# First feed-forward's down product: two by two blocks in seven products instead of eight, with the sums of blocks made on GpSimd during the up phase

## The reference

```python
h2 = rms_norm(x, norm2_g[l])
up = h2 @ w_up[l]                                  # 1024 -> 2 * 2816
up = causal_depthwise_conv(up, ffn_dw_w[l])        # 3 taps
gate, val = jnp.split(up, 2, axis=-1)
x = x + (jax.nn.silu(gate) * val) @ w_down[l]      # 2816 -> 1024
```

## Time and profile before

| | |
|---|---|
| median of 3 runs | 2790.98 us (2790.71 to 2793.44) |
| profiled execution, its time | 2792.19 us |
| its span | 2790.6 us |
| granted TensorE clock over the span | 0.993 |
| TensorE busy | 2728.8 us (98%) |
| VectorE busy | 1754.9 us (63%) |
| GpSimd busy | 642.3 us (23%) |

### The profile page before, as it was taken

How to read it: one execution, slowest core, us unless ns; L and a number is a source line. 1 busy time by engine, 2 the same in 40 slices (tenths; PEclk the granted TensorE clock), 3 DMA queues, 4 the chain that set the end, 5 groups by cost and what they waited for, 6 DMA issues and landing times.

```text
span 2790.6 us, 32012 instructions
## 1 busy us (share of the span) xinstructions
PE 2728.8 (98%) x12499; PEld 2211.9 (79%) x12499; DVE 1754.9 (63%) x2235; ACT 1122.7 (40%) x1582; POOL 642.3 (23%) x548
## 2 busy tenths in 40 slices
PE   9999999999999999999999999999999999999997
PEld 6877667788888788888878888766777888888886
DVE  6776554589999853233324444576547787776567
ACT  4322543343333443221235565665345322223543
POOL 1213111001101053011002222113423244444013
PEclk9999999999999999999999999999999999999999
DMA  3215532334444474334622233566543365657773
GB/s 123 78 67 157 132 94 91 139 99 136 116 122 129 140 248 144 121 136 150 226 91 88 72 102 93 168 187 187 196 167 125 134 215 186 204 191 244 267 249 128
DMA packets 147285, 414.49 MB, mean 149 GB/s; under 512 B 18616, under 2 KB 23352, under 8 KB 147136
## 3 DMA queue, kind: packets, MB, share of 16 engines
q1 hardware_dynamic: 115024, 309.97, 34.3%
q0 software_dynamic: 32112, 102.48, 12.0%
HBM read 309.46 MB, written 102.92 MB: 148 GB/s over the span
## 4 chain that ended last, share of the span: by engine, by line
PE 82%; DVE 9%; ACT 4%; issue 2%; DMA 2%; POOL 1%; SPq 0%; DVEq 0%; POOLq 0%; ACTq 0%
PE ps L218 80%; DVE cacc L189 1%; ACT PB L183 1%; PE ps L221 1%; POOL ga L186 1%; DVE PB L189 1%; DVE cv L189 1%; DVE tl L186 0%; DVE YA L186 0%; DMA raw<-in_w_win 0%; DVE AL L189 0%; DVE stk L186 0%; DVE sqacc L186 0%; DVE wl L186 0%; ACT gt L183 0%
## 5 line engine op out<-in xcount | busy, mean ns | idle before, releaser
L218 PE MATMUL ps<-AH,wh 128*128 128x512 f32 (+1 forms) x1104 | 446.5, 404 | 19.1 <-DVE T L186 5.7
L218 PE MATMUL ps<-AH,wl 128*128 128x512 f32 (+1 forms) x1104 | 432.2, 391 | 0.0
L218 PE MATMUL ps<-AL,wh 128*128 128x512 f32 (+1 forms) x1104 | 431.6, 391 | 0.0
L218 PEld LDWEIGHTS ps<-AH,wh 128*128 128x128 f32 (+1 forms) x1104 | 206.6, 187 | 73.5 <-issue 13.1
L218 PE MATMUL ps<-stk,stk 128*128 128x512 f32 (+3 forms) x832 | 242.2, 406 | 11.9 <-DVE small L198 5.9
L218 PEld LDWEIGHTS ps<-AH,wl 128*128 128x128 f32 (+1 forms) x1104 | 206.5, 187 | 46.5
L218 PEld LDWEIGHTS ps<-AL,wh 128*128 128x128 f32 (+1 forms) x1104 | 207.0, 188 | 44.5 <-issue 2.9
L218 PEld LDWEIGHTS ps<-stk,stk 128*128 128x128 f32 x832 | 146.7, 190 | 80.1 <-issue 32.6
L186 DVE TENSOR_TENSOR wl<-raw,wh 128x1024 fp32r<-128x1024 f32 (+1 forms) x76 | 112.7, 1484 | 150.9 <-ACT wh L183 135.8
L218 PE MATMUL ps<-euh,ewt 128*128 128x512 f32 x640 | 197.9, 389 | 1.3 <-DVE eul L186 1.3
L186 POOL TENSOR_TENSOR wl<-raw,wh 128x1024 fp32r<-128x1024 f32 (+3 forms) x47 | 102.5, 2181 | 324.4 <-ACT wh L183 324.3
(11 more groups left out here) (321 smaller groups left out, 6395.0 us busy)
## 6 DMA issues: line engine op xcount, KB each, us to landing
ewr<-in_dn SPq DMA_DIRECT2D x88, 256.0 KB, 3.1
pwr<-in_w_up SPq DMA_DIRECT2D x38, 512.0 KB, 4.2
swr<-in_w_gu SPq DMA_DIRECT2D x38, 512.0 KB, 4.3
raw<-in_w_w2in SPq DMA_DIRECT2D x32, 512.0 KB, 4.2
scr_u<-cv SPq DMA_DIRECT2D x22, 512.0 KB, 2.6
eur<-scr_u SPq DMA_DIRECT2D x44, 256.0 KB, 3.2
scr_u<-uu SPq DMA_DIRECT2D x22, 512.0 KB, 9.6
alr<-in_dn POOLq DMA_DIRECT2D x11, 1024.0 KB, 10.3
```

The source lines that it names most:

```text
L218: return Issued(self, self.e.matmul(out, l, r, start=start, stop=stop, skip_group_check=onto))
```

## The change

The 88 steps of the first feed-forward's down product become 77: seven products of blocks, 11 steps each. The sums of weight blocks and of gated blocks are made by GpSimd in the loop that issues `added`: after `added(n)` comes one `weight_sums` (even n) or one `block_sums` (odd n), and three more after the loop. Each is a load of 1 MB into the one area `TW1`, four additions of 128x512 in place, and a store of 1 MB to scratch; each waits until the store before it has landed, since both kinds use the same area. `TW1` lies where the fourth part of the token sums was (`tl1` reaches 4 when that is done) and where two of the 22 places for gated blocks are; those two are now numbers 20 and 21, and their loads wait for the last store. Gated blocks are loaded at every step (77 instead of 44). VectorE makes the low parts of the first 22, GpSimd those of the other 55. `evacuate` subtracts eight times four results instead of four times four.

```diff
+        self.TW1 = Area(nc, sq, sq + 8192).get("tw1", [P, 4, 512])
...
-        for w in range(88):
-            p, k = w // 22, w % 22
+        for w in range(7 * NK):
+            p, k = w // NK, w % NK
             q.wait_ge(S.dwl1, w + 1)
-            q.wait_ge(S.dul1, 22 * (p // 2) + k + 1)
-            if k == 0:
-                q.wait_ge(S.fe1, 4 * (p - 1))
+            q.wait_ge(S.dul1, w + 1)
+            if k == 0 and p > 1:
+                self.e_freed(q, p - 2)
...
+            for n, half in self.INTO1[p]:
+                x = self.XR[:, n + j, HALF[half]]
+                q.tt(x, x, self.d_bank(p, j), ALU.subtract).then_inc(S.fe1)
...
+        def weight_sums(j):
+            q.wait_ge(S.tl1, 4)
+            q.wait_ge(S.jd1, 32 * j)
+            q.dma(self.TW1[:, :, :], self.io["dn1"][2 * j:2 * j + 2, :, :, :].rearrange("i h p c -> p (i h) c")).then_inc(
+                S.jl1, 16)
+            a11, a21, a12, a22 = [self.TW1[:, x, :] for x in range(4)]
+            q.wait_ge(S.jl1, 48 * j + 16)
+            q.tt(a22, a21, a22, ALU.add).then_inc(S.jb1)
...
+            q.tt(a12, a12, a11, ALU.subtract).then_inc(S.jb1)
+            q.wait_ge(S.jb1, 8 * j + 4)
+            q.dma(self.io["s_s1"][j, :, :, :], self.TW1[:, :, :]).then_inc(S.jd1, 16)
+
+        def block_sums(j):
+            q.wait_ge(S.jd1, 32 * j + 16)
+            q.wait_ge(S.du1, 32 * j + 32)
+            for x in range(2):
+                q.dma(self.TW1[:, 2 * x:2 * x + 2, :], self.io["s_u1"][2 * j + x, :, :].rearrange("p (h t) -> p h t", t=512)).then_inc(
+                    S.jl1, 16)
...
+            q.dma(self.io["s_t1"][j, :, :, :], self.TW1[:, :, :]).then_inc(S.jd1, 16)
+
         for n in range(NQ):
             added(n)
-        q.wait_ge(S.dul1, 10)
-        for u in range(10, 22):
-            u_low(u)
...
+            if n % 2:
+                block_sums(n // 2)
+            else:
+                weight_sums(n // 2)
+        block_sums(9)
+        weight_sums(10)
+        block_sums(10)
+        q.wait_ge(S.dul1, 22)
+        for u in range(22, 7 * NK):
             u_low(u)
+            if 53 <= u < 56:
+                summed(0, u - 52)
...
+            if u in (20, 21):
+                q.wait_ge(S.jd1, 32 * NK)
+            if kind == "t":
+                q.wait_ge(S.jd1, 32 * k + 32)
+                src = self.io["s_t1"][k, :, at[0], :]
...
-        for w in range(9, 88):
+        for w in range(9, 7 * NK):
             d_load(w)
-            if w < 21:
+            if w < 7 * NK - 1:
                 u_load(w + 1)
```

More of the change, by code:

```diff
@@ L381, in __init__ @@
         self.EU, self.EUR, self.EU_FREE = [], [], []
[L382 to L389, removed]
+        homes = [("g", k, 0, 1) for k in range(4)] + [("g", 4, 0, 2), ("g", 5, 0, 2), ("g", 4, 1, 5), ("g", 5, 1, 5)]
+        homes += [("a", k, 1, 7) for k in (0, 1, 2)] + [("a", 6, 1, 7), ("a", 7, 1, 7)]
+        homes += [("a", k, 1, 7) for k in (4, 5, 3)] + [("g", k, 1, 7) for k in range(4)]
         for which, k, half, free in homes:
@@ L395, in __init__ @@
             self.EU_FREE.append(free)
+        for x in range(2):
+            one = Area(nc, sq + 4096 * x, sq + 4096 * x + 4096)
+            self.EUR.append(Area(nc, one.lo + 2048, one.hi).get("eur", [P, 512])[:, :])
+            self.EU.append(tuple(one.get("eu", [P, 512], F32R)[:, :] for _ in range(2)))
+            self.EU_FREE.append(7)
+        self.TW1 = Area(nc, sq, sq + 8192).get("tw1", [P, 4, 512])
         w = Area(nc, lo + 4096, TOP)
@@ L1558 @@
     SHAPE1 = [("X11", 0), ("X21", 1), ("T2", 5), ("T1", 4), ("X22", 6), ("T3", 2), ("T4", 3)]
-    E_FREE = {slot: max(w for w in range(88) if w % DW == slot) for slot in range(DW)}
+    INTO1 = [((0, 1),), ((0, 0), (4, 0)), ((0, 0),), ((0, 0),), ((4, 0),), ((0, 1),), ((4, 1),)]
+    E_SLOT = [w % DW for w in range(74)] + [6, 7, 8]
+    E_FREE = {slot: max(w for w in range(77) if w < 74 and w % DW == slot or w == 68 + slot > 73) for slot in range(DW)}
     def f1_tile(self, x):
@@ L1644, in pe_ff1 @@
                 part(n, i)
[L1646 to L1647 removed]
+        for w in range(7 * NK):
+            p, k = w // NK, w % NK
             q.wait_ge(S.dwl1, w + 1)
[L1649 to L1653 removed]
+            q.wait_ge(S.dul1, w + 1)
+            if k == 0 and p > 1:
+                self.e_freed(q, p - 2)
+            wh, wl = self.EWT[self.E_SLOT[w]]
+            uh, ul = self.EU[w % 22]
+            first, onto = k == 0 and p in (0, 1, 3, 5), p in (2, 4, 6)
             for n in range(4):
@@ L1658, in pe_ff1 @@
                 out, ws = self.d_bank(p, n), slice(n * P, n * P + P)
[L1659 to L1662, removed]
+                q.mm(out, wh[:, ws], uh, first, False, onto)
+                q.mm(out, wh[:, ws], ul, False, False, onto)
+                t = q.mm(out, wl[:, ws], uh, False, k == NK - 1, onto)
+                if k == NK - 1:
                     t.then_inc(S.dn1)
-            if k < 21:
+            if k < NK - 1:
                 t.then_inc(S.dk1)
@@ L1788, in square @@
                 q.act(self.sqF[n % 2][:, :], self.XR[:, n, c], ACT.Square).then_inc(S.ps if t else S.sF)
[L1790 to L1802, removed]
+        for w in range(6, 7 * NK):
+            d_high(w)
+            u_high(w)
+            for p in (3, 4):
+                if 0 <= w - NK * (p + 1) - 8 < 4:
+                    n = 4 * (p - 3) + w - NK * (p + 1) - 8
+                    square(0, n)
+                    into(0, n)
+            if 72 <= w < 76:
+                square(1, w - 72)
         for n in range(4):
@@ L2007, in into @@
                   ALU.subtract).then_inc(S.pl)
[L2009 to L2012, removed]
+        for w in range(6, 7 * NK):
+            d_low(w)
+            if w < 22:
                 u_low(w)
[L2014 to L2018, removed]
+            for p in range(5):
+                if 0 <= w - NK * (p + 1) - 7 < 4:
+                    evacuate(p, w - NK * (p + 1) - 7)
+                if p > 2 and 0 <= w - NK * (p + 1) - 10 < 4:
+                    into(0, 4 * (p - 3) + w - NK * (p + 1) - 10)
+            if 71 <= w < 75:
+                evacuate(5, w - 71)
         for n in range(4):
@@ new lines, in block_sums @@
+        def block_sums(j):
+            q.wait_ge(S.jd1, 32 * j + 16)
+            q.wait_ge(S.du1, 32 * j + 32)
+            for x in range(2):
+                q.dma(self.TW1[:, 2 * x:2 * x + 2, :], self.io["s_u1"][2 * j + x, :, :].rearrange("p (h t) -> p h t", t=512)).then_inc(
+                    S.jl1, 16)
+            b12, b11, b22, b21 = [self.TW1[:, x, :] for x in range(4)]
+            q.wait_ge(S.jl1, 48 * j + 48)
+            q.tt(b11, b12, b11, ALU.subtract).then_inc(S.jb1)
+            q.wait_ge(S.jb1, 8 * j + 5)
+            q.tt(b12, b22, b12, ALU.subtract).then_inc(S.jb1)
+            q.wait_ge(S.jb1, 8 * j + 6)
+            q.tt(b22, b22, b11, ALU.subtract).then_inc(S.jb1)
+            q.wait_ge(S.jb1, 8 * j + 7)
+            q.tt(b21, b21, b22, ALU.subtract).then_inc(S.jb1)
+            q.wait_ge(S.jb1, 8 * j + 8)
+            q.dma(self.io["s_t1"][j, :, :, :], self.TW1[:, :, :]).then_inc(S.jd1, 16)
@@ L2070, in pool_ff1 @@
+        block_sums(10)
+        q.wait_ge(S.dul1, 22)
+        for u in range(22, 7 * NK):
+            u_low(u)
+            if 53 <= u < 56:
+                summed(0, u - 52)
+            if 63 <= u < 67:
+                summed(0, u - 59)
+            if u == 74:
+                summed(1, 1)
+        for n in range(2, 4):
             summed(1, n)
@@ L2254, in dve_proj2 @@
             scale = {"qa": 0.125 * 4.0 ** key[1], "qb": 0.125}
-            q.stt(self.T2[b][:, :], self.pair(b), scale[key[0]] if key[0] in scale else 1.0, self.RB[:, :], ALU.mult,
+            q.stt(self.T2[b][:, :], self.pair(b if n > 1 else 2 + b), scale[key[0]] if key[0] in scale else 1.0, self.RB[:, :], ALU.mult,
                   ALU.mult).then_inc(S.bev)
```

101 lines of the change are left out of this document (56 added, 45 removed), and 4 rows, old and new, of the table SHARED.

## The result

The changed kernel takes 2837.59 us (median of four runs, 2832.27 to 2842.05), the kernel before 2791.57 beside it: a ratio of 1.0163, 95% interval 1.0147 to 1.0180. Forecast were 2835 us. The profiled span is 2834.9 us against 2790.6. The sum holds; apart from the matmuls saved, none of its terms measured what was forecast, and one that was counted as costing nothing turned out to be the bound for most of the stage. The page's busy times first: TensorE has 132 matmuls less, and its share falls from 98 to 96%.

What follows compares the result with a forecast made beforehand. TensorE, busy 98%, was taken to bound the kernel before, GpSimd's round the changed up phase. 46.9 + 17.5 + 9.4 - 29.9 = 43.9 us slower, added to 2790.98, gave 2835 us; range 2795 to 2880.

Steps and rivals of the forecast that it cites:

- matmuls saved: Down phase, 88 steps become 77: 132 matmuls of 0.2267 us go, 29.9 us gained.
- late start: Start of up phase: first sum delays `added(1)`, so TensorE's turn 1 begins at 625.5 instead of 608.07, 17.5 us once.
- 17 turns: Up phase, `added(1)` to `added(18)`: each round takes 21.8 us against a turn of 19.04, 46.9 us lost.
- end: Down phase near step 20: load of gated block 20 waits for the last sum, 9.4 us lost.
- GpSimd's round: Up phase: store, load and four additions take 21.8 us and set the turn; 20.5 to 23.5 us given chance 0.62.
- Contention: Up phase: GpSimd's additions stretch VectorE by 1.07 us per turn, to 19.3 us, costing nothing under a 21.8 us round.
- the rival's doubt: Up phase: 13.4 of VectorE's 18.2 us can collide, without the idle 20% of the second feed-forward.
- the hope that additions meet operations on TensorE's results: Up phase: GpSimd adds about 4 us after VectorE's weight sums, where operations reading TensorE's results stand thickest.
- VectorE becomes the bound: Rival, up phase: each addition costs VectorE 1.15 us, turn 22.8 us, 2852 us in all; chance 0.13.
- A round that fits the turn: Rival, up phase: faster transfers give a round of 16.6 us, 2766 us in all; chance 0.13 (below 2785).
- a round of 25.3 us by slower transfers: Rival, up phase: transfers slower still, 2908 us in all; chance 0.08 (above 2880).
- The turn of 24.9 us: Up phase: by the skill's exclusion rule in full, four additions of 1.67 us would add 6.7 us to VectorE's turn.

Runs made afterwards that it cites:

- e1: Changed kernel with GpSimd's four additions per sum kept, but each sum's load and store cut to 8 KB: 2826.51 us, 1.0119 of the kernel before.
- e6: Changed kernel with only the block sums made, weight sums left out and weight blocks taken as they are: 2788.77 us, 0.9991 of the kernel before.
- e3: Changed kernel with the accumulating DMAs `added(n + 1)` issued ahead of sum n instead of behind it: 2836.74 us, 1.0162 of the kernel before.
- e4: Changed kernel with SP's loads of the down phase's first four steps issued ahead of a gated-block store: 2829.95 us, 1.0136 of the kernel before.
- e5: Changed kernel with each sum's load and store kept, its four additions replaced by fills of 64 columns: 2777.89 us, 0.9952 of the kernel before.

## Why the prediction was right, and where not

| term | forecast, us | measured, us |
|---|---|---|
| matmuls saved | -29.9 | -29.9 (taken as such) |
| late start | +17.5 | +13.3 |
| 17 turns | +46.9 | +41.0 |
| end | +9.4 | +17.9 |
| the same code ahead and behind | 0 | -3.5 + 5.5 |
| sum | +43.9 | +44.3 |

Measured by TensorE's starts in the two profiled executions (the medians of the runs differ by 46.0). The sum is within 0.4 us of the forecast because a late start and turns that were 10.1 us cheaper stand against an end and outer code that were 10.5 us dearer: that is luck. Start: turn 1 begins 25.19 us after the wait for the last token sum, 11.92 before. Turns: 364.7 us against 17 x 19.04 = 323.7. End: from turn 18 to the first wait after the stage 275.2 us against 287.2, 12.0 less where 29.9 were saved. The two numbers outside the stage belong to code that is the same; behind the stage the experiments' spans leave between 1573.0 and 1581.2 us, and the two kernels 1571.6 and 1577.1. What makes them differ stays open.

**The turn.** "So GpSimd's round, and no longer TensorE, sets the turn" can hold for turns 2 to 7 at most; from turn 8 on VectorE sets it. The turn came out near 21.8 all the same, at 21.45, and that is luck too: VectorE's limit happens to lie there. GpSimd's round itself was near, at 20.9, with errors against each other: on average of its 17 rounds a load took 7.0 us until the additions and not 9.0, while four additions took 7.9 us and not 6.9, because GpSimd waits in collisions too.

**Contention** is the term that was mis-sized: 1.07 us per turn, and "costs nothing". From 700 to 900 us VectorE works 0.98 x 21.45 = 21.0 us per turn instead of 0.952 x 19.04 = 18.1: 2.9 us. The price of one collision in the rival was right (1.15, measured 1.1), and the rival's doubt as well: no idle 20% here. What was wrong was the carrying over of an average from the second feed-forward, whose VectorE is idle for 20% of the time: there 19 of 54 additions from 2250 to 2500 us stretch an operation, here 56 of 64 and in e1 all. Wrong as well was the hope that additions meet operations on TensorE's results: at 785.02 they begin 1.3 us after VectorE's weight sums, not 4, amid the low parts. Here 2.9 us (3.0 in e1, 3.3 in e6) of 4 x 1.1 are paid, two thirds to three quarters, since nearly every addition hits but is partly over when VectorE's operation begins. The rival "VectorE becomes the bound" was the truer mechanism, at 21.4 us a turn and not 22.8. A round that fits the turn (faster) or a round of 25.3 us by slower transfers are both excluded by the 20.9 us measured.

The Trainium skill ("SBUF — State Buffer", section "Who interferes with whom") has the right pairing: a VectorE instruction with two SBUF inputs against a GpSimd instruction that reads SBUF, not one that only writes. The traces agree on each part: 0.68 us unchanged on operations with one operand in PSUM, 1217 ns under fills, 1.78 instead of 0.69 under additions. That the second waits for the whole of the first, as the prediction took the rule, is borne out too: each stretched operation is through 0.13 to 0.20 us less than its undisturbed time after GpSimd's instruction. The turn of 24.9 us that the prediction worked out by it did not come for other reasons: its 1.67 us for an addition already held GpSimd's own waiting (alone it takes 1.27), and VectorE pays only for the part of an addition that is left when its operation begins, 0.77 us on average.

**The start** was 4.2 us cheaper because the first load and the first additions were quicker (12.47 us to `added(1)` instead of 16.75); from there to TensorE's turn it took 12.7 us, as forecast. That it is "once, since a loop that is itself the bound never catches up" was true for another reason: e3 shows that the chain of the 22 sums passes it on to the end.

**The end** came out twice as long, and from other causes. The wait near step 20 is 0.58 us, since the stage began late enough to cover it. In its place SP's loads stood behind the store of a late gated block (6.5 us, of which e4 leaves 2.8), the next low parts were late (8.1 us, six times) behind loads of up to 8.5 us and, at 1028.08, behind operations stretched by additions, and the lower granted clock around these waits made up most of the rest: the waits are 12.3 us more than before, and 40 us at 0.87 lack 5.2 us of full clock. The prediction followed SP's queue at `u_load(20)` and not at its first load.

**The price of transfers** was rightly no bound of its own (e5), and the other 55 low parts on GpSimd and the 77 steps cost nothing that the trace shows.

## What to carry to other kernels

Before moving work to an idle engine, count what it reads from the memory that the busy engine reads too: the idle engine's time is free, its reads aren't. Take the price of a collision from single stretched instructions and count on nearly every read meeting one where the busy engine has no gaps; an average of a stage with slack hides that. And where a serial chain runs through a whole stage, follow it to its last consumer: a wait removed at its start may only come back at its end.

## What was not expected of the hardware

A 128x512 float32 addition on GpSimd costs VectorE up to 1.10 us in an operation with two operands in SBUF (0.69 to 1.78, 1.22 to 2.32), a copy of that size up to 0.41 us, a fill of 128x2048 nothing. The stretched operation ends about its undisturbed time after the end of GpSimd's instruction, so the two take turns and do not share. GpSimd pays as well: 1.27 us alone, 2.14 at the median. Doubling the DMA traffic to 237 GB/s changed no duration of VectorE.
